# A hybrid mLSTM/MLA encoder layer: both feed-forward blocks by one level of Strassen products

## What is computed

```python
def rms_norm(x, g):
    y = x * lax.rsqrt(jnp.mean(x * x, axis=-1, keepdims=True) + EPS)
    return y * g

def swiglu_half(x, pre_g, w_gate, w_up, w_down, post_g):
    h = rms_norm(x, pre_g)
    u = jax.nn.silu(h @ w_gate) * (h @ w_up)
    return x + 0.5 * rms_norm(u @ w_down, post_g)
```

## Time and profile before

| | |
|---|---|
| median of 3 runs | 1323.68 us (1320.59 to 1332.14) |
| profiled execution, span from first to last instruction | 1324.1 us |
| TensorE busy / granted clock, mean | 97% / 0.983 |
| block 1, first product to last | 18.1 to 453.7 us |
| mixer, first product to last | 463.7 to 853.9 us |
| block 2, first product to last | 863.6 to 1301.1 us |

### The profile page before, as it was taken

The page is one execution under the profiler, slowest core; times in us unless marked ns, Lnnn a source line. Parts: engine busy times, 40 slices in busy tenths (PEclk is TensorE's granted clock), DMA queues, the critical chain, the costliest instruction groups (busy, mean ns, idle before and its releaser), DMA issues.

```text
span 1324.1 us, 22215 instructions
## 1 busy us (share of the span) xinstructions
PE 1282.1 (97%) x9238; PEld 1228.8 (93%) x9238; DVE 511.1 (39%) x716; ACT 406.6 (31%) x630; POOL 148.0 (11%) x158
## 2 busy tenths in 40 slices
...
DMA packets 188273, 94.61 MB, mean 71 GB/s; under 512 B 17403, under 2 KB 187728, under 8 KB 188224
## 3 DMA queue, kind: packets, MB, share of 16 engines
q1 hardware_dynamic: 187120, 92.06, 24.8%
...
q10 hardware_dynamic: 16, 0.00, 0.0%
...
## 4 chain that ended last, share of the span: by engine, by line
PE 94%; DVE 3%; DMA 1%; ACT 1%; issue 1%; SPq 0%; POOL 0%; POOLq 0%; ACTq 0%; DVEq 0%
PE PS L339 81%; PE PS L357 3%; PE PS L1593 2%; PE PS L1564 2%; PE PS L1579 1%; PE PS L371 1%; PE PS L1287 1%; DMA XIN<-in_x_prompt 1%; PE PS L942 1%; DVE Y L399 0%; PE PS L1275 0%; DVE DW L1434 0%; PE PS L1268 0%; POOL X L412 0%; DVE X L402 0%
## 5 line engine op out<-in xcount | busy, mean ns | idle before, releaser
L339 PE MATMUL PS<-H_HI,W_HI 128*128 128x288 f32 (+1 forms) x1760 | 381.2, 298 | 8.2 <-DVE H_LO L457 8.0
L319 ACT ACTIVATE W_HI<-RAW 128x1024 fp32r<-128x1024 f32 (+2 forms) x187 | 180.5, 965 | 670.2 <-PE PS L339 670.2
L339 PE MATMUL PS<-H_LO,W_HI 128*128 128x288 f32 (+1 forms) x1760 | 378.1, 296 | 0.0
L339 PE MATMUL PS<-H_HI,W_LO 128*128 128x288 f32 (+1 forms) x1760 | 377.9, 296 | 0.0
L323 DVE TENSOR_TENSOR W_LO<-RAW,W_HI 128x1024 fp32r<-128x1024 f32 (+2 forms) x187 | 208.8, 1117 | 290.2 <-ACT W_HI L319 290.2
L339 PEld LDWEIGHTS PS<-H_HI,W_HI 128*128 128x128 f32 (+1 forms) x1760 | 283.6, 189 | 10.1 <-issue 9.2
L339 PEld LDWEIGHTS PS<-H_HI,W_LO 128*128 128x128 f32 (+1 forms) x1760 | 284.3, 189 | 0.0
L339 PEld LDWEIGHTS PS<-H_LO,W_HI 128*128 128x128 f32 (+1 forms) x1760 | 284.2, 189 | 0.0
L339 PE MATMUL PS<-U_HI,W_HI 128*128 128x288 f32 x704 | 150.8, 296 | 0.0
L339 PE MATMUL PS<-U_LO,W_HI 128*128 128x288 f32 x704 | 150.7, 296 | 0.0
L339 PE MATMUL PS<-U_HI,W_LO 128*128 128x288 f32 x704 | 150.7, 296 | 0.0
...
## 6 DMA issues: line engine op xcount, KB each, us to landing
RAW<-in_ff_w_gate SPq DMA_DIRECT2D x44, 512.0 KB, 3.8
RAW<-in_ff_w_up SPq DMA_DIRECT2D x44, 512.0 KB, 3.8
...
RAW<-in_w_in SPq DMA_DIRECT2D x21, 512.0 KB, 3.8
...
RAW<-in_w_out SPq DMA_DIRECT2D x8, 512.0 KB, 3.9
XIN<-in_x_prompt SPq DMA_DIRECT2D x4, 512.0 KB, 6.9
out<-XIN SPq DMA_DIRECT2D x4, 512.0 KB, 3.0
```

What stands on the lines that cost most here:

```text
L319: nc.scalar.activation(W_HI[:, b % NW, 0:n, :], raw_slot(b)[:, 0:n, :], ACT.Copy).then_inc(w_hi, 1)
L339: last = nc.tensor.matmul(PS[0:m, bank + s, 0:n], w, x[:, s * n:(s + 1) * n], start=start and i == 0, stop=stop and i == 2)
```

## The change

Each weight matrix pair (gate tile over up tile, or four quarters of the down matrix) and each activation (two halves of the features, two halves of the frames) is seen as a 2 x 2 block matrix, and the four block results come from 7 products of quarters in place of 8, in Winograd's form: sums of weight quarters (S1 to S4) and of activation quarters (T1 to T4) go in, and results are put together from products kept in PSUM.

A block is a list of 38 jobs, written out without loops. A gate/up job ("g", one j) is 7 products of 4 tiles x 3 passes = 84 matmuls of 288 columns. A down job ("d", chunk c, a quarter q of the outputs) is 7 products over the pairs of u tiles in its chunk: 42 matmuls with two pairs (chunk 0), 63 with three. Chunks are worked off as their u is ready, so u is kept for three pairs only; their contributions are added up in X, and X itself is written to DRAM at the start of the block (`spill_x`) and read back as XOLD into the place of H once the last gate/up job has used that.

For each job and product i: POOL forms the four weight sums in SB (`weight_sums`); ACT makes WQ_HI and DVE WQ_LO (`weight_hi`, `weight_lo`, 128 x 512 in a g job); TensorE multiplies. Products 0, 2, 4 and 6 go to bank_a, 1 and 5 to bank_c, 3 to bank_b. ACT copies a partial result out (`snap`: SNS, SNQ) before the bank is added to further, and DVE adds snapshot and bank: ev11 (G, the first gate half), ev22, ev21. Product 2 waits for snapshot 0, product 4 for snapshot 2, product 6 for ev22. When the second step of a pair is through, POOL forms four sums of u (`u_sums`), and ACT and DVE split all seven operands (`u_high`, `u_low`) in the job after it; before the last chunk this stands ahead of the job (`urgent`). In down jobs of chunks 1 to 3 DVE adds the bank to X and POOL adds the snapshot (`y_add`).

The input factor is now applied before the products: squares and root of the whole X first (block 1: ACT on the loaded rows; block 2: ACT squares, TensorE sums), then HF = X x gain x factor, TH the four sums, HHI and HLO the seven operands (`h_factors`). Loads of x come first in SP's queue. After the mixer, X additions alternate between DVE and POOL; after block 1 all eight stay on POOL (`fpost_pool`, against XOLD). The load of TRIG moves from POOL's start to `cache_pool`, and `cache_pool` now stands behind the additions.

```diff
-MIX0 = NB_FF
+
+
+NP = JF // 2
+CHUNKS = ((0, 2), (2, 5), (5, 8), (8, 11))
+JOBS = []
+for _c, (_lo, _hi) in enumerate(CHUNKS):
+    _first = 0 if _c == 0 else 2 * _lo + 1
+    _last = min(2 * _hi + 1, JF)
+    JOBS += [("g", _j, 0) for _j in range(_first, _last)]
+    JOBS += [("d", _c, _q) for _q in range(KD // 2)]
...
+                                 dv[:, 2 * lo:2 * hi, 2 * q * P:2 * (q + 1) * P]).then_inc(f["raw"][s].sem, 16)
+                if r == 1:
+                    spill_x()
+            sp.wait_ge(*f["used"].at(NPROD * (GJOB[JF - 1] + 1)))
+            sp.wait_ge(*f["moved"].at(16))
+            sp.dma_start(XOLD[:].rearrange("p k t -> p (k t)"), spill).then_inc(f["moved"].sem, 16)
+
...
+        def ffn_pe(pe, f, e):
+            for r, (kind, x, q) in enumerate(JOBS):
...
+                    if i == 2:
+                        pe.wait_ge(*f["snap"].at(3 * r + 1))
...
+                    if i == 4:
+                        pe.wait_ge(*f["snap"].at(3 * r + 3))
+                    if i == 6:
+                        pe.wait_ge(*f["ev22"].at(r + 1))
...
+                    for k in range(n):
+                        if kind == "g":
+                            hi, lo = HHI[:, i, k, :], HLO[:, i, k, :]
+                        else:
+                            hi, lo = UHI[:, k, U_OF[i], :], ULO[:, k, U_OF[i], :]
+                        wh, wl = WQ_HI[:, i, k * P:(k + 1) * P], WQ_LO[:, i, k * P:(k + 1) * P]
+                        for s, (w, h) in enumerate(passes(wh, wl, hi, lo)):
+                            last = nc.tensor.matmul(PS[:, bank, 0:HT], w, h, start=i in (0, 1, 3) and k == 0 and s == 0,
+                                                    stop=k == n - 1 and s == 2, skip_group_check=True)
+                    last.then_inc(f["used"].sem, 1)
...
+        def snap(act, f, r, n):
+
+            act.wait_ge(*f["used"].at(NPROD * r + n + 1))
+            if r:
+                kind, x, q = JOBS[r - 1]
+                if kind == "d" and x:
+                    act.wait_ge(*f["yp"].at(3 * gates(x, q) + n + 1))
+                else:
+                    act.wait_ge(*(f["ev11"], f["ev22"], f["ev21"])[n].at(r))
+            bank = (BANKS[r % 2][0], BANKS[r % 2][2], BANKS[r % 2][0])[n]
+            nc.scalar.activation((SNS[:, 0], SNS[:, 1], SNQ[:])[n], PS[:, bank, 0:HT], ACT.Copy).then_inc(f["snap"].sem, 1)
...
+        def weight_hi(act, f, r, i):
...
+            if r:
+                act.wait_ge(*f["used"].at(NPROD * (r - 1) + i + 1))
+            n = width(r)
+            if i in S_OF:
+                act.wait_ge(*f["s_done"].at(4 * r + S_OF[i] + 1))
+                src = wide(SB[:, S_OF[i]], n)
+            else:
+                act.wait_ge(*f["raw"][r % 2].at(landed(r)))
+                src = quarters(r)[{0: 0, 3: 1, 5: 3}[i]]
+            nc.scalar.activation(wide(WQ_HI[:, i], n), src, ACT.Copy).then_inc(f["w_hi"].sem, 1)
...
+            n = width(r)
+            dve.wait_ge(*f["w_hi"].at(NPROD * r + i + 1))
+            src = wide(SB[:, S_OF[i]], n) if i in S_OF else quarters(r)[{0: 0, 3: 1, 5: 3}[i]]
+            nc.vector.tensor_tensor(wide(WQ_LO[:, i], n), src, wide(WQ_HI[:, i], n).bitcast(F32),
...
+        def weight_sums(pool, f, r):
...
+            n = width(r)
+            pool.wait_ge(*f["raw"][r % 2].at(landed(r)))
+            a11, a12, a21, a22 = quarters(r)
+            s3, s1, s2, s4 = (wide(SB[:, s], n) for s in range(4))
+            if r:
+                pool.wait_ge(*f["w_lo"].at(NPROD * (r - 1) + 2))
+            nc.gpsimd.tensor_tensor(s3, a11, a21, ALU.subtract).then_inc(f["s_done"].sem, 1)
+            if r:
+                pool.wait_ge(*f["w_lo"].at(NPROD * (r - 1) + 5))
+            nc.gpsimd.tensor_tensor(s1, a21, a22, ALU.add).then_inc(f["s_done"].sem, 1)
+            pool.wait_ge(*f["s_done"].at(4 * r + 2))
+            nc.gpsimd.tensor_tensor(s2, s1, a11, ALU.subtract).then_inc(f["s_done"].sem, 1)
+            if r:
+                pool.wait_ge(*f["w_lo"].at(NPROD * (r - 1) + 7))
+            pool.wait_ge(*f["s_done"].at(4 * r + 3))
+            nc.gpsimd.tensor_tensor(s4, a12, s2, ALU.subtract).then_inc(f["s_done"].sem, 1)
+
+        H_SRC = (HF[:, 0:4, 0:HT], TH[:, 0], TH[:, 2], HF[:, 4:8, 0:HT], TH[:, 1], TH[:, 0], HF[:, 4:8, HT:T])
...
+        def u_high(act, f, p):
+            s = slot_of(p)
+            u_free(act, f, p)
+            act.wait_ge(*f["ut"].at(4 * p + 4))
+            nc.scalar.activation(UHI[:, s, 0], u_tile(p, 0), ACT.Copy).then_inc(f["u_hi"].sem, 1)
+            nc.scalar.activation(UHI[:, s, 1:3], UF[:, p % 2, 1].rearrange("p (a n) -> p a n", a=2),
+                                 ACT.Copy).then_inc(f["u_hi"].sem, 1)
+            act.wait_ge(*f["tu"].at(4 * p + 4))
+            nc.scalar.activation(UHI[:, s, 3:7], TU[:], ACT.Copy).then_inc(f["u_hi"].sem, 1)
+
...
+        def u_sums(pool, f, p):
+            pool.wait_ge(*f["ut"].at(4 * p + 4))
+            if p:
+                pool.wait_ge(*f["u_lo"].at(3 * p))
+            nc.gpsimd.tensor_tensor(TU[:, 0], u_tile(p, 3), u_tile(p, 1), ALU.subtract).then_inc(f["tu"].sem, 1)
+            nc.gpsimd.tensor_tensor(TU[:, 1], u_tile(p, 1), u_tile(p, 0), ALU.subtract).then_inc(f["tu"].sem, 1)
+            pool.wait_ge(*f["tu"].at(4 * p + 2))
+            nc.gpsimd.tensor_tensor(TU[:, 2], u_tile(p, 3), TU[:, 1], ALU.subtract).then_inc(f["tu"].sem, 1)
+            pool.wait_ge(*f["tu"].at(4 * p + 3))
...
+                if urgent(r):
+                    u_high(act, f, done_pair(r))
+                    nc.scalar.activation(WARM[:], EPSC[:], ACT.Sqrt)
+                for n in range(3):
+                    snap(act, f, r, n)
+                    weight_hi(act, f, r + 1, n)
+                if kind == "g":
+                    act.wait_ge(*f["ev11"].at(r + 1))
+                    nc.scalar.activation(G[:, 0], G[:, 0], ACT.Silu).then_inc(f["silu"].sem, 1)
+                weight_hi(act, f, r + 1, 3)
+                if done_pair(r) is not None and not urgent(r):
+                    u_high(act, f, done_pair(r))
+                if kind == "d" and x == len(CHUNKS) - 1 and q:
+                    y_square(act, f, p, q - 1, 0)
+                    y_square(act, f, p, q - 1, 1)
...
+            for k in range(KD):
+                g = GROW[gain] + k
+                nc.vector.scalar_tensor_tensor(out=HF[:, k], in0=X[:, k], scalar=GCOLS[:, g:g + 1], in1=spread_at(PRE_SPREAD),
+                                               op0=ALU.mult, op1=ALU.mult).then_inc(e["hf"].sem, 1)
+                if k == 3:
+                    if not early:
+                        weight_lo(dve, f, 0, 0)
+                    h_lo(dve, e, 0)
+            dve.wait_ge(*e["hf"].at(KD))
+            nc.vector.tensor_tensor(TH[:, 0], HF[:, 4:8, HT:T], HF[:, 0:4, HT:T], ALU.subtract).then_inc(e["th"].sem, 1)
+            if not early:
+                weight_lo(dve, f, 0, 1)
+            h_lo(dve, e, 1)
...
+                if urgent(r):
+                    u_low(dve, f, done_pair(r))
+                for i in range(3):
+                    weight_lo(dve, f, r + 1, i)
+                dve.wait_ge(*f["used"].at(NPROD * r + 4))
+                dve.wait_ge(*f["snap"].at(3 * r + 1))
+                if kind == "g":
...
+                    nc.vector.tensor_tensor(G[:, 0], SNS[:, 0], pb, ALU.add).then_inc(f["ev11"].sem, 1)
...
+                weight_lo(dve, f, r + 1, 3)
+                dve.wait_ge(*f["used"].at(NPROD * r + 5))
+                dve.wait_ge(*f["snap"].at(3 * r + 2))
...
+                    nc.vector.tensor_tensor(u2, SNS[:, 1], pa, ALU.add).then_inc(f["ev22"].sem, 1)
...
+                weight_lo(dve, f, r + 1, 4)
+                dve.wait_ge(*f["used"].at(NPROD * r + 6))
+                dve.wait_ge(*f["snap"].at(3 * r + 3))
+                if kind == "g":
+                    nc.vector.tensor_tensor(u1, SNQ[:], pc, ALU.add).then_inc(f["ev21"].sem, 1)
+                    dve.wait_ge(*f["ev21"].at(r + 1))
+                    dve.wait_ge(*f["silu"].at(2 * x + 1))
+                    nc.vector.tensor_tensor(u1, u1, G[:, 0], ALU.mult).then_inc(f["ut"].sem, 1)
...
+                if done_pair(r) is not None and not urgent(r):
+                    u_low(dve, f, done_pair(r))
...
+                weight_lo(dve, f, r + 1, 5)
+                if kind == "g":
+                    dve.wait_ge(*f["silu"].at(2 * x + 2))
+                    dve.wait_ge(*f["ev22"].at(r + 1))
+                    nc.vector.tensor_tensor(u2, u2, G[:, 1], ALU.mult).then_inc(f["ut"].sem, 1)
...
+                weight_lo(dve, f, r + 1, 6)
...
+        def fpost_pool(pool, f, e):
+            pool.wait_ge(*f["moved"].at(32))
+            for k in range(1, KD, 2) if e is fpost[1] else range(KD):
+                pool.wait_ge(*e["t"].at(k + 1))
+                nc.gpsimd.tensor_tensor(X[:, k], X[:, k], XOLD[:, k], ALU.add).then_inc(e["x"].sem, 1)
...
+        def y_add(pool, f, r, n):
+
+            _, x, q = JOBS[r]
```

(51 more changed lines are left out.)

690 lines of the change are left out of this document (407 added, 283 removed).

## The result

The changed kernel takes 1482.93 us (median of 4 runs, 1479.3 to 1484.95) against 1322.72 us of the kernel before beside it: ratio 1.119 (95% interval 1.116 to 1.123), slower by 160 us. I had forecast 1399 us with a range up to 1445: the direction was right, the size was not. The profiled execution spans 1481.6 us.

The account below looks back on a forecast made before the run. The prediction took TensorE, busy 97% of 1324.1 us, as the bound. It summed -105.7 + 68 + 40 + 10 + 20 + 3 + 20 + 17 + 2.5 = +74.8 to 1399 us, range 1300 to 1445.

Parts of the forecast that it names:

- -105.7 for the matmuls: Both blocks: 3168 matmuls each become 2772, at an unchanged 0.1334 us per matmul, saving 105.7 us.
- clock rival: Rival: stalls let TensorE's clock fall to 1.2 GHz in the pieces between, +40 on the sum, 1439 us; chance 0.12.
- Turns on the port: DVE instructions with two SBUF operands and POOL instructions take turns: 22.6 us per gate/up pair against TensorE's 22.4.
- Gate/up pairs, +68: Late ev22 delays product 6: 4.2 us per pair inside a run, 1.8 at its edge, +68 us.
- Down jobs, +40 and +10: Snapshots late behind y_add and weight sums in three-pair jobs, +40 us (12 to 60); two-pair jobs +10 (3 to 15).
- Urgent pair, +20: Before the last down chunk: TensorE idles 9.2 us for u sums and splits, restarts slowly; +20 us both blocks (12 to 24).
- Starts of the blocks, +3 and +17: Input factor before products, then the ramp of seven: block 1 +3 us (0 to 8), mixer to block 2 +17 (10 to 24).
- Block 1 to mixer, +20: Cache loads behind POOL's X additions delay the transposes that begin the mixer: +20 us (12 to 26).
- Tail, +2.5: The end of the kernel after block 2: +2.5 us.
- Queues keep up: Rival: ev22 and snapshots always beat TensorE's product, so only fixed terms stay, 1287 us; chance 0.16.
- Full but work-conserving: Rival: port full but no bubbles from queue order, about 1 us a pair, 1324 us, no change; chance 0.12.
- Successive matmuls in one bank: Rival: accumulating in one bank successively is slower than two banks in turn, 5.5 us per ns per matmul; no chance given.

Follow-up runs that it names:

- e1: Changed kernel with POOL's weight sums and u sums replaced by memsets of constants that read nothing (layer not computed): 1355.47 us, ratio to before 1.023.
- e10: Changed kernel with cache loads, y_add, u_high/u_low and ramp snapshots all reordered, plus all weight and u sums on DVE instead of POOL: 1360.78 us, ratio 1.027.
- e5: Changed kernel with u_high and u_low behind the job's last weight split in gate/up jobs that a gate/up job follows: 1457.59 us.
- e12: e10 with u_high and u_low back at their first place, between splits 3 and 4 on ACT and ahead of split 5 on DVE: 1390.06 us.
- e3: Changed kernel with POOL's y_add placed between the weight sums of job r+2 in down jobs of chunks 1 to 3, not behind them: 1433.45 us.
- e6: Changed kernel with job 0's three ACT snapshots between the h_hi, and DVE adding ev11 and ev22 ahead of the next job's splits: 1473.0 us.
- e2: Changed kernel with the loads of CIN, KIN and TRIG ahead of the eight X additions in POOL's queue, TRIG last: 1468.44 us.
- e4: Changed kernel with spare matmuls on TensorE where it idles, in gate/up and down jobs and ahead of chunks' first down products: 1483.05 us.
- e11: Changed kernel with cache loads, y_add, u_high/u_low and ramp snapshots all reordered, plus spare matmuls ahead of product 6 and first down products: 1379.94 us.

## Why the prediction was right and wrong

The terms, by the table, miss 83 us in all. The direction and the mechanism (turns on the port, late evacuations behind a full queue) were right. Three steps failed: the rate of the products that was kept at 0.1334 us, "the ramp of seven takes some 25 us", and norm sums before block 2 that were to keep up with the squares.

- **-105.7 for the matmuls: right in count, wrong in rate.** In e1 whole gate/up runs stand at 11.2 us a job, so unit and shape keep the rate. But "Shape and passes stay, so I keep the rate" put slower products at nothing, and TensorE's busy time fell by 37 us only. What that cost is in the down jobs and under the clock rival.
- **Turns on the port: right, and decisive.** Splits take 0.86 to 1.02 us on the mean; e1 and e10 bring them back to 0.7. The Trainium skill (SBUF — State Buffer, the section on two separate sides) calls the shared pair an exclusive lock held for the whole instruction. POOL's 2.88 us sum beside three full-speed splits agrees.
- **Gate/up pairs, +68: measured 78.** In-run pairs lose 3.7 us, expected 4.2, nearly all in one job of the two. That u_high's place is part of it is shown (e5, e12), that it is nearly all of it (3.6 of 4.2, I had said) is not: moving it takes away 1.4 of 3.7. What I missed are the last jobs of a run, 3.2 to 5.7 us each where I had 1.8, because the wait for ULO (4.1 us on the mean, six times) stands at every chunk, not only at the last. I had put that wait at the urgent pair alone.
- **Down jobs, +40 and +10: measured 69 and 19, the largest single miss.** The wait was as forecast: 20 waits for a snapshot, 2.1 us each on the mean, 42 us, and e3 takes 50 of the 69 away. What failed is the rate. Of the 69 us 41 are idle time and some 27 are products slower than 0.1334 us a matmul, at a mean granted clock of 0.92 (the rest is bookkeeping: a period takes in product 0 of the next job, and that of a gate/up job is wider). Whether the slow products would cost anything without the waits stays open: e3 takes both away. Jobs so lost not 1.6 to 3 but 1.9 to 4.7 us, and more of them: the last of chunks 1 and 2, with a gate/up job behind it, lost 3.9 to 4.7. Of the 19 us of the two-pair jobs 14 lie in the last one of each block's first chunk, 4 us of each being a wait for DVE's addition to X.
- **Urgent pair, +20: 24.4.** The wait is 10.4 us in place of 9.2.
- **Starts of the blocks, +3 and +17: short by 11 and 17.** "The ramp of seven takes some 25 us" failed: it took 34.6 us in block 1 and 31.5 in block 2, from the first product on. I added up splits and h_lo and overlooked that product 2 waits for a snapshot that stands behind the whole ramp in ACT's queue; e6, which moves it, wins 10 us in all. The longer ramp is nearly all of block 1's miss, but only 6.5 us of block 2's. There the first product itself came 37.6 us after the mixer's last, where I had 27.1. X was ready on time (16.9 us after it, forecast 17.1), but the norm sums did not keep up. The window, TensorE and ACT in the changed kernel (columns as in the earlier trace rows):
```profile
935.00:955.00 20.00, 19.84 (x80) 16.45 (x80) 8.24 (x10) 4.69 (x8) 5.61 (x4) 0.51 0.28 119
```
```profile
929.03 1.53 PE L366 MATMUL PS<-ONES,PAIR 128*128 128x96 f32 x10
...
935.16 5.04 PE L366 MATMUL PS<-ONES,PAIR 128*128 128x96 f32 x20 [2.35 <-ACT PAIR L931]
...
949.85 5.14 PE L366 MATMUL PS<-ONES,PAIR 128*128 128x96 f32 x20
```
```profile
944.85 0.68 ACT L931 ACTIVATE PAIR<-X 128x576 f32<-128x576 f32 x1 [1.46 <-POOL X L415]
```
  Behind the pauses the granted clock is at its lower level, 1.2 GHz (0.51 in the window); twenty sums take 5.14 us where ten took 1.53, and the last ends at 954.99, 9.5 us after the last square. At the speed of the row at 929.03 it would have ended near 947, an estimate: 8 us. Another 1.3 us went when POOL's TH sum and DVE's first HLO took turns (the HLO at 962.66 takes 2.68 us in place of 1.36). No run here filled these pauses.
- **Block 1 to mixer, +20: right**, +24.6 in the gap less 6.6 in a shorter mixer; e2 shows the cause. **Tail, +2.5: +6.6.** After the pause for the last squares the norm sums run slowly:
```profile
1455.22 2.79 PE L366 MATMUL PS<-ONES,ACC 128*128 128x96 f32 x10 [3.21 <-DVE ACC L798]
```
  the same ten took 1.50 us right behind dense work in the kernel before.
- **The clock rival came true in its condition and not in its price.** Mean 0.91 to 0.92 in the blocks; my argument against it, that dense work follows each pause, did not hold. But lifting it inside the blocks gives 0 (e4) and 10 us (e11): in most jobs DVE and POOL set the pace. Both runs also lengthen some pauses by the spare matmuls, so that the exact share stays open. At the seams it had a price, the 8 us above and some in the tail, and neither run touches those.
- **The range, up to 1445, was too narrow for its own terms.** Their upper ends add up to 1477 us. Five of the seven terms with a range came out above its upper end: both kinds of down job, the urgent pair (by 0.4 us), and both starts.
- *Queues keep up*: false, ev22 was late in 18 jobs. *Full but work-conserving*: false, order alone is worth 93 us. *Successive matmuls in one bank*: false, 84 in 11.2 us.

Against the list of signs: splits and sums above 0.69 and 1.25, the 20 us before the transposes of CIN, and ev22 late in every second job all stood there; in-run pairs took 24 to 27 us, and the wait before the last chunk 10.4.

Open are these: why the sums shift their price between DVE and POOL from turn to turn; what the lower clock costs by itself in the down jobs and at the seams; and whether e10 with ramps and seams laid out anew would win (48 us of what it adds lie outside the jobs, and it is 37 over the kernel before). The last wasn't tried.
